# One fused two-block kernel: the first stage's projections as a stream of split weight units, x loaded first, norm sums gathered on VectorE, the memory chain placed inside the projections

## The chip, the cores and the metric

The kernel runs on one core of one Trainium2 chip. The metric is device time in microseconds (us) of one execution. The kernel works on five engines that run side by side and meet at semaphores: TensorE (PE; its weight loads are listed as PEld), VectorE (DVE), ScalarE (ACT), GpSimd (POOL) and SyncE (SP, which here only issues DMAs).

## The reference

Two transformer-like blocks follow one another on x (512 tokens x 1024). The change touches only the part of the first block ahead of its experts:

```python
mem_n = rms_norm(mem, mem_norm_w)                 # mem: 256 x 1024
h = rms_norm(x, ln1_w)
proj = h @ w_in                                   # 1024 x 2560: xr, xg, q, k, v (512 columns each)
y_rnn = recurrent_group(xr, xg, ...)              # conv of width 4, two gates, a linear recurrence, gelu gate
y_att = chunk_band_attention(q, k, v, rel_bias)   # 8 heads of 64
mixed = concat([rms_norm(y_rnn, gn_rnn_w), rms_norm(y_att, gn_att_w)])
x = x + mixed @ w_out
h = rms_norm(x, ln2_w)
# cross-attention to mem_n, 4 heads of 256: q = h @ wq, k = mem_n @ wk, v = mem_n @ wv, then @ wo
x = x + memory_cross_attention(h, mem_n, wq, wk, wv, wo)
h = rms_norm(x, ln3_w)
x = x + hierarchical_moe(h, ...)                  # 32 experts, top 2 of a group; then a final norm
# then two layers of the second block: projections, four mixers, w_out, and a feed-forward part
```

## The kernel before, in words

Activations lie transposed: features on the 128 partitions, the 512 tokens along the free dimension, so a vector of 1024 features is 8 chunks of 128x512. All weights come from DRAM in fp32.

The kernel has three stages. The first is everything up to the router, the second the experts (a loop over blocks of 128 slots), the third the two layers of the second block. The experts and the layers already multiply in split form: each fp32 weight tile and each activation is written as a high part (a copy in the fp32r type) and a low part (the difference), and three fp32r matmuls (high x high, high x low, low x high) stand for one fp32 matmul. In the layers a *unit* is 8 chunks x 256 columns of a weight (1 MB). `unit_high` (ACT, line 1201) and `unit_low` (DVE, line 1193) split it into one of two buffers `split_weights0/1` (`WHL`). `unit_high(g)` waits for the DMA of unit g and for PE to be done with unit g-2; PE waits for `weights_low` (`wl_done`) of unit g. The DMA of unit g is issued on SP once unit g-2 is split.

The first stage does none of that. It uses plain fp32 matmuls straight from the ring of three 2 MB buffers (`ring`, `first_uses`): `project` (line 1910) makes four output tiles of 128x512 from one 512-column weight block, `tokens` (line 1922) makes token-major tiles. PE's order is: stats of mem and of x, K and V of the memory (2+2 blocks), the five blocks of `w_in`, with the two gate matmuls of the recurrence (line 1945) behind each tile of the third, attention in 16 pairs (`pe_pairs`), the stats of the two group norms, `w_out`, stats, `xq`, cross-attention (`pe_attention`), `xo`, stats, router. Each stat (`pe_stats`, line 1674) multiplies all 4 or 8 squared chunks by a matrix of ones. ACT takes the results out of the banks (line 2080), squares chunks, and makes 1/root (`act_rstd`: Ln at line 2056, Exp at 2057, each with a table load). DVE does the norms (`dve_norm`, 1977), the conv, the recurrence, the softmax work and the residual adds (1983).

SP issues konst, cols, mem, two weight blocks, then x, then the other blocks, each when its ring buffer is free. POOL prepares the relative bias (through DRAM, into `AUX`) and later writes 16.8 MB of zeros to `expert_rows` (line 362), once 28 tiles are done.

Each engine works its list in order: an instruction that waits holds up all that is behind it on that engine.

Of the kernel before, what the change touches and what calls it, by code (L numbers as in the profile page):

```python
# [17 lines left out]
ALU = mybir.AluOpType  # L18
# [62 lines left out]
NORMS = [("mem", DC), ("ln1", DC), ("gn_rnn", HC), ("gn_att", HC), ("ln2", DC), ("ln3", DC), ("final", DC)]  # L81
# [28 lines left out]
def build(nc, A, out):  # L110
    with ExitStack() as ctx:
# [12 lines left out]
        with ExitStack() as places:  # L124
# [8 lines left out]
            QP = place("split_products_low", [P, 16, T])  # L133
        ring = [sb(f"ring{i}", [P, 8, 512]) for i in range(RING)]
# [31 lines left out]
        MT = S[:, 16:20, :].rearrange("p a (b m) -> p (a b) m", m=MEM)  # L166
# [3 lines left out]
        s_x = sem("x_landed")  # L170
# [4 lines left out]
        w_landed = [sem(f"weights_landed{i}") for i in range(RING)]  # L175
        act_own, dve_own, pool_own = sem("act_steps"), sem("dve_steps"), sem("pool_steps")
        sq_done, stat_done, rstd_done, h_done = sem("squares"), sem("stat"), sem("rstd_done"), sem("h_chunks")
        tile_done, tile_free = sem("tile_done"), sem("tile_free")
        xc_done, gate_done, gate_free = sem("conv_done"), sem("gates_done"), sem("gates_free")
# [5 lines left out]
        chunks_before = {}  # L185
        n = 0
        for i, (name, c) in enumerate(NORMS):
            chunks_before[name] = (i, n, c)
            n += c


        def wblock(w, j):
            return w[j]


        first_uses = [(wblock(A["xk_w"], j), tile_done, 4 * j + 4) for j in range(2)]
        first_uses += [(wblock(A["xv_w"], j), tile_done, 8 + 2 * j + 2) for j in range(2)]
        first_uses += [(wblock(A["w_in"], j), tile_done, 12 + 4 * j + 4) for j in range(5)]
        first_uses += [(wblock(A["w_out"], j), res_done, 4 * j + 4) for j in range(2)]
        first_uses += [(wblock(A["xq_w"], j), tile_done, 32 + 4 * j + 4) for j in range(2)]  # L200
        first_uses += [(wblock(A["xo_w"], j), res_done, 8 + 4 * j + 4) for j in range(2)]
        assert len(first_uses) % RING == 0
# [14 lines left out]
        for j in range(HEADS // 2):  # L217
            for t in range(TT):
# [4 lines left out]
                    bias=[AUX[:, h, T - keys:T] for h, r, tt in halves(j, t)],  # L223
# [88 lines left out]
        def wait_counted(eng, sem_, value):  # L312

            eng.wait_ge(sem_, value)
            eng.sem_inc(counted_waits, 1)

        def moe_sync(sp):
            sp.wait_ge(*first_uses[-3][1:])
            sp.wait_ge(*first_uses[-2][1:])
            sp.wait_ge(*first_uses[-1][1:])  # L320
            sp.wait_ge(slots_done, 1)
# [1935 lines left out]
```

## Time and profile before

| | us |
|---|---|
| three runs | 2636.82 median (2635.71 to 2639.95) |
| the profiled execution, whole | 2646.86 |
| its span, first to last instruction | 2645.2 |
| start to first projection matmul | 43.82 |
| last V tile done, attention begins | 243.15 |
| attention's last output copied | 313.27 |
| `w_out` done | 385.72 |
| first matmul of `xq` | 397.20 |
| `xq` done | 454.10 |
| `xo` starts | 489.82 |
| `xo` done | 545.06 |
| router starts | 561.17 |

PE is busy 88% of the span, DVE 57%, ACT 41%. The times in the lower rows are places in the chain of work that ended last, in us from the span's start. Behind the router the change only merges semaphores.

### The profile page before, as it was taken

The numbers are of one execution on the slowest core, as the hardware profiler recorded it, in microseconds if no ns is written. First come the engines' busy times: TensorE is split into PE (matmuls) and PEld (weight loads), VectorE is DVE, ScalarE is ACT, GpSimd is POOL, SyncE is SP. The second block draws the span as 40 slices with busy tenths as digits, with TensorE's granted clock in tenths as the row PEclk, the third lists the DMA queues.
The fourth block names the chain that finished last, engine by engine and source line by source line (L and its number), as shares of the span: only waits on it lengthen the run. The fifth ranks groups of instructions, "written<-read, shape, count | busy, mean of one in ns | idle before, by whom it ended". The sixth has DMA issues, their size and how long they took to land.

```text
span 2645.2 us, 26498 instructions
## 1 busy us (share of the span) xinstructions
PE 2322.3 (88%) x9824; PEld 1692.4 (64%) x9824; DVE 1507.1 (57%) x1851; ACT 1096.5 (41%) x1335; POOL 196.4 (7%) x158
## 2 busy tenths in 40 slices
PE   5998799964888888888569788999998979899997
PEld 4444444643777777776437466888877647688885
DVE  1104511233788788877556767646556785764565
ACT  2123511213666666666344564222224563422223
POOL 1000000001000000000100100211110010120110
PEclk8998799976999999999879899999999999999998
DMA  6317010006999999999612101322322101222221
GB/s 260 122 69 278 40 64 32 1 32 214 334 362 360 359 354 359 363 357 355 262 34 86 42 1 64 106 101 84 108 96 82 62 33 42 79 102 98 88 103 48
DMA packets 50454, 399.15 MB, mean 151 GB/s; under 512 B 6560, under 2 KB 7768, under 8 KB 24896
## 3 DMA queue, kind: packets, MB, share of 16 engines
q1 hardware_dynamic: 32992, 336.12, 35.3%
q0 software_dynamic: 12192, 42.97, 4.2%
q10 hardware_dynamic: 5184, 18.88, 1.7%
q8 instruction: 59, 0.97, 0.1%
q14 instruction: 27, 0.22, 0.0%
HBM read 360.15 MB, written 40.41 MB: 151 GB/s over the span
## 4 chain that ended last, share of the span: by engine, by line
PE 68%; DVE 12%; ACT 10%; issue 6%; DMA 3%; ACTq 1%; POOL 0%; SPq 0%; DVEq 0%; POOLq 0%
PE bank L987 36%; PE bank L1910 11%; PE bank L436 8%; DVE split_products L576 3%; ACT split_products L666 2%; ACT split_x_high L666 2%; PE bank L1922 2%; PE bank L1674 2%; DVE split_x_low L576 2%; PE bank L426 1%; PE bank L1704 1%; ACT S L1768 1%; PE bank L1689 1%; PE bank L1718 1%; DMA X<-in_xT 1%
## 5 line engine op out<-in xcount | busy, mean ns | idle before, releaser
L987 PE MATMUL bank<-split_x_high,split_weights 128*128 128x512 f32 x2144 | 672.9, 394 | 36.3 <-DVE split_x_low L1207 14.7
L987 PEld LDWEIGHTS bank<-split_x_high,split_weights 128*128 128x128 f32 x2144 | 408.0, 190 | 128.2 <-issue 42.7
L1201 ACT ACTIVATE split_weights<-ring 128x2048 fp32r<-128x2048 f32 (+1 forms) x92 | 170.9, 1859 | 523.2 <-PE bank L987 522.0
L987 PE MATMUL bank<-split_products,split_weights 128*128 128x512 f32 x1200 | 334.6, 395 | 4.5 <-DVE split_products L1393 4.5
L987 PE MATMUL bank<-split_x_low,split_weights 128*128 128x512 f32 x800 | 312.6, 391 | 0.0
L1910 PE MATMUL bank<-H,ring 128*128 128x512 f32 x640 | 278.1, 595 | 4.8 <-DVE H L1977 3.6
L987 PEld LDWEIGHTS bank<-split_products,split_weights 128*128 128x128 f32 x1200 | 229.3, 191 | 54.1 <-DVE split_products L1393 6.0
L1193 DVE TENSOR_TENSOR split_weights<-ring,split_weights 128x2048 fp32r<-128x2048 f32 (+1 forms) x92 | 207.9, 2260 | 94.6 <-ACT split_weights L1201 94.6
L436 PE MATMUL bank<-split_products,split_products_low 128*128 128x512 f32 x768 | 195.8, 405 | 70.2 <-DVE split_products L576 70.2
L1910 PEld LDWEIGHTS bank<-H,ring 128*128 128x128 f32 x640 | 121.9, 191 | 159.6 <-issue 155.1
L436 PEld LDWEIGHTS bank<-split_products,split_products_low 128*128 128x128 f32 x768 | 146.4, 194 | 113.6 <-DVE split_products L576 82.8
L576 DVE TENSOR_TENSOR split_products<-ring,split_products 128x2048 fp32r<-128x2048 f32 x64 | 146.7, 2292 | 109.2 <-ACT split_products L666 109.2
L436 PE MATMUL bank<-split_x_high,split_products_low 128*128 128x512 f32 x768 | 193.5, 402 | 7.0 <-DVE split_x_high L576 4.9
L436 PE MATMUL bank<-split_x_low,split_products_low 128*128 128x512 f32 x768 | 190.6, 398 | 8.5 <-DVE split_x_low L576 8.5
L666 ACT ACTIVATE split_products<-ring 128x2048 fp32r<-128x2048 f32 x64 | 122.8, 1918 | 122.0 <-DVE QKVG L588 69.4
L987 PEld LDWEIGHTS bank<-split_x_low,split_weights 128*128 128x128 f32 x800 | 151.1, 189 | 31.3
L576 DVE TENSOR_TENSOR split_x_high<-ring,split_x_high 128x2048 fp32r<-128x2048 f32 x64 | 146.5, 2289 | 40.9 <-ACT split_x_high L666 40.9
L436 PEld LDWEIGHTS bank<-split_x_high,split_products_low 128*128 128x128 f32 x768 | 145.4, 193 | 37.5 <-issue 7.6
L436 PEld LDWEIGHTS bank<-split_x_low,split_products_low 128*128 128x128 f32 x768 | 144.2, 191 | 37.6 <-DVE split_x_low L576 8.7
L965 POOL TENSOR_TENSOR QKVG<-QKVG 128x512 f32<-128x512 f32 x44 | 97.8, 2223 | 810.5 <-DVE QKVG L1407 723.9
L576 DVE TENSOR_TENSOR split_x_low<-ring,split_x_low 128x2048 fp32r<-128x2048 f32 x64 | 146.2, 2285 | 5.3 <-ACT split_x_low L666 5.3
L666 ACT ACTIVATE split_x_high<-ring 128x2048 fp32r<-128x2048 f32 x64 | 122.0, 1906 | 30.4 <-DMA ring<-in_expert_gate_w 19.8
(360 smaller groups left out, 2687.4 us busy)
## 6 DMA issues: line engine op xcount, KB each, us to landing
ring<-in_expert_gate_w SPq DMA_DIRECT2D x32, 2048.0 KB, 10.9
ring<-in_expert_up_w SPq DMA_DIRECT2D x32, 2048.0 KB, 8.8
ring<-in_expert_down_w SPq DMA_DIRECT2D x32, 2048.0 KB, 10.6
ring<-in_ffn_w_up SPq DMA_DIRECT2D x44, 1024.0 KB, 4.9
expert_rows<-nothing POOLq DMA_DIRECT2D x4, 4096.0 KB, 35.7
expert_rows<-QKVG ACTq DMA_DIRECT2D x32, 512.0 KB, 10.1
ring<-in_w_in SPq DMA_DIRECT2D x16, 1024.0 KB, 4.9
ring<-in_ffn_w_down SPq DMA_DIRECT2D x16, 1024.0 KB, 4.8
```

Of the source, the lines that this page charges most:

```text
L426: mm = pe.transpose(bank[4 + j][:, c * P:(c + 1) * P], XB[:, (4 * j + c) * P:(4 * j + c + 1) * P], ident)
L436: mm = pe.matmul(acc[j][:, :], xs[i][:, (u % 2) * n_k + k, :], w[:, n_j * k + j, :], start=(u % 2 == 0 and k == 0 and q == 0), stop=(u % 2 ...
L576: dve.tensor_tensor(e_low(u), e_raw(u), as_f32(e_high(u)), ALU.subtract).then_inc(ew_low, 1)
L666: act.activation(e_high(u), e_raw(u), ACT.Copy).then_inc(ew_high, 1)
L965: st.tell(pool.tensor_tensor(QKVG[:, 14 + i, :], QKVG[:, b, :], QKVG[:, 4 + b, :], ALU.mult), f_act)
L987: mm = pe.matmul(acc[:, :], w[:, u, k, m], x, start=first and q == 0, stop=last and q == 2)
L1193: st.tell(dve.tensor_tensor(w[:, 1, 0:ks, 0:nc_], raw_half(g)[:, :, 0:nc_], as_f32(w[:, 0, 0:ks, 0:nc_]), ALU.subtract), wl_done)
L1201: st.tell(act.activation(WHL[g % 2][:, 0, 0:ks, 0:nc_], raw_half(g)[:, :, 0:nc_], ACT.Copy), wh_done)
L1674: mm = pe.matmul(acc[:, 0:n], ones, src(c), start=(c == 0), stop=(c == chunks - 1))
L1689: pe.matmul(bank[2 * (p % 2) + i][:, 0:x["keys"]], q, k, start=True, stop=True).then_inc(s["scored"], 1)
L1910: mm = pe.matmul(b[:, 0:n], w[:, k, m * P:(m + 1) * P], src(k), start=(k == 0), stop=(k == DC - 1))
L1922: mm = pe.matmul(b[:, :], src(k)[:, t * P:(t + 1) * P], w[:, k, :], start=(k == 0), stop=(k == DC - 1))
```

## The change

All 30 MB of first-stage weights become 30 units of 256 columns (`A_UNITS`: `w_in` 10, `xk` 4, `xv` 4, `w_out` 4, `xq` 4, `xo` 4), at the head of the list of units that the layers already have. PE multiplies in three fp32r matmuls where it had one fp32 matmul. `split_unit` makes two tiles of 128x512 per unit (128x256 for the memory's K); `token_unit` makes token-major tiles, whose moving side is now the 256 columns of the unit instead of 512.

The activations are split as well: ACT copies each normed chunk (`high`), DVE subtracts (`normed_split`). x is loaded first, in four pieces; mem is loaded behind the first two units. The squares are summed on DVE (into `LN1[0]` or `SUM`), so that the matmul with ones runs over 1 to 3 chunks, not 4 or 8. K and V of the memory move behind all of `w_in`; the norm of mem, the lambda terms and `unit_high`/`unit_low` are spread over ACT's and DVE's lists. The norm of the recurrence's output is done ahead of attention. With `together=True` a unit's two tiles advance chunk by chunk as chunks are ready. Work inside attention (`inside`) takes the splitting of the recurrence's output and the square sums of the attention's. The bias goes to `H` instead of `AUX`, later (after 24 tiles); the copy of the bias in DRAM waits for 4 tiles. Semaphores of the stages are merged.

```diff
+A_UNITS = (("w_in", 10), ("xk_w", 4), ("xv_w", 4), ("w_out", 4), ("xq_w", 4), ("xo_w", 4))
@@ SP
+            for i in range(4):
+                sp.dma_start(X[:, 2 * i:2 * i + 2, :].rearrange("p a t -> p (a t)"), A["xT"][:, 2 * T * i:2 * T * (i + 1)]).then_inc(s_x[i], 16)
             sp.dma_start(konst[:, :], A["konst"]).then_inc(s_const, 16)
             sp.dma_start(cols[:, :], A["cols"]).then_inc(s_const, 16)
...
+            for g in range(UA):
+                if g >= 2:
+                    sp.wait_ge(wl_done, g - 1)
+                sp.dma_start(raw_half(g).rearrange("p k n -> p (k n)"), unit_source(g)).then_inc(half_landed[g % 2], 16)
+                if g == 1:
+                    sp.dma_start(MT.rearrange("p k m -> p (k m)"), A["memT"]).then_inc(s_mem, 16)
@@ POOL
+            pool.wait_ge(tile_done, A_XK)
+            pool.dma_start(BIAS, bass.AP(ext_copies.tensor, ...
@@ PE
+            def split_unit(g, n0, done, free, count, n=T, before=None, order=tuple(range(DC)), together=False):
+                pe.wait_ge(wl_done, g + 1)
+                w = WHL[g % 2]
...
+                def product(i, k):
+                    for q, (u, x) in enumerate(((0, hi(k)), (0, lo(k)), (1, hi(k)))):
+                        mm = pe.matmul(accs[i][:, 0:n], w[:, u, k, i * P:(i + 1) * P], x, start=(k == order[0] and q == 0), stop=(k == order[-1] and q == 2))
+                    return mm
...
+            def token_unit(g, n0, tt, hi, lo):
...
+                            mm = pe.matmul(bank[(n0 + t) % 4][:, 0:256], x[:, tok], w[:, u, k, :], start=(k == 0 and q == 0), stop=(k == DC - 1 and q == 2))
...
+            rms("ln1", ((a_add, 5, LN1[0]), (a_sq, 7, LN1[6]), (a_sq, 8, LN1[7])))
...
+            split_unit(0, **tiles(0), count=xin, before=lambda k: pe.wait_ge(a_lo, k + 1), together=True)
+            split_unit(1, **tiles(2), count=xin)
+            pe.wait_ge(side_dve, 1)
+            pe.matmul(bank[4][:, 0:MEM], ones, MSUM, start=True, stop=True).then_inc(mem_stat, 1)
+            split_unit(2, **tiles(4), count=xin)
...
+            for g in range(4, 8):
+                split_unit(g, **tiles(2 * g), count=xin)
+            token_unit(8, A_V, TT, *xin)
+            token_unit(9, A_V + TT, TT, *xin)
...
+            for u in range(4):
+                split_unit(10 + u, **tiles(A_XK + 2 * u), count=mem_in, n=MEM)
+            rms("gn_rnn", ((a_add, 8, SUM),))
+            for u in range(4):
+                token_unit(14 + u, A_XV + 2 * u, 2, *mem_in)
+            pe.wait_ge(tile_free, A_XQ)
             pe_pairs(pe, att_cfg[0], 0)
...
+            rms("gn_att", ((a_add, 10, SUM), (a_sq, 16, square[1])))
+            split_unit(18, **res(0), count=mixed, before=lambda k: pe.wait_ge(a_lo, DC + k + 1), together=True)
@@ PE, values of cross-attention
-                        pe.wait_ge(s["att_out"], outs + need)
+                    if x["t"] == 0 and u:
+                        pe.wait_ge(cross_low, outs_before(cfg, u))
@@ DVE
+            unit_low(dve, st, 2)
+            conv(0)
+            conv(1)
+            dve.wait_ge(side_act, 1)
+            st.tell(dve.tensor_reduce(MSUM, MSQ.rearrange("p k m -> p m k"), AX.X, ALU.add), side_dve)
...
+            unit_low(dve, st, 12)
+            unit_low(dve, st, 13)
+            dve.wait_ge(a_rstd, 2)
+            for c in range(HC):
+                st.tell(dve.scalar_tensor_tensor(G[:, c, :], G[:, c, :], col("gn_rnn", c), rstd[:, :], ALU.mult, ALU.mult), a_hn)
+            for g in range(14, 20):
+                unit_low(dve, st, g)
@@ ACT
+            unit_high(act, st, 10)
+            for t in range(TT):
+                evac(V[:, t, 0:256], half)
+            unit_high(act, st, 11)
+            for t in range(TT):
+                evac(V[:, t, 256:512], half)
...
+            for u in range(4):
+                unit_high(act, st, 12 + u)
+                for c in range(2 * u, 2 * u + 2):
+                    evac(KM[:, c, :], half)
+            root(1, HC)
+            for u in range(4):
+                unit_high(act, st, 16 + u)
+                for t in range(2):
+                    evac(VM[:, t, u * 256:(u + 1) * 256], half)
```

The order of instructions, at the places that matter. First the head of PE's list. Before: stats of mem (`S` times the ones in `konst`), stats of x, then the memory's K from `ring`.

```order
L1674 MATMUL bank<-S,konst 128x256 [waits squares,const_landed]
L1674 MATMUL bank<-S,konst 128x256 [waits squares] x7
L1674 MATMUL bank<-H,konst 128x512 [waits squares,rstd_done]
L1674 MATMUL bank<-H,konst 128x512 [waits squares] x7
L1910 MATMUL bank<-S,ring 128x256 [waits h_chunks,weights_landed0]
```

And after: the stats of x in three matmuls, then unit 0 chunk by chunk (six matmuls each).

```order
L1910 MATMUL bank<-S,konst 128x512 [waits x_squares_added,const_landed]
L1910 MATMUL bank<-S,konst 128x512 [waits x_squares] x2
L1876 MATMUL bank<-split_x_high,split_weights 128x512 [waits x_normed_low,weights_low]
L1876 MATMUL bank<-split_x_low,split_weights 128x512
L1876 MATMUL bank<-split_x_high,split_weights 128x512 x2
```

The stats and projections of the memory have left the head of the list. Second, DVE's list around the norm of the recurrence's output (`QKVG` times `rstd`), after; the rows with `split_weights` are `unit_low` of units 12, 13, then 14 to 19, and the last one is the first of attention.

```order
L2097 TENSOR_TENSOR ext<-ext,gatew 128x512 [waits x_squares_added,x_squares] x2
L1164 TENSOR_TENSOR split_weights<-ring,split_weights 128x2048 [waits weights_high] x2
L2106 SCALAR_TENSOR_TENSOR QKVG<-QKVG,cols,rstd 128x512 [waits x_rstd]
L2106 SCALAR_TENSOR_TENSOR QKVG<-QKVG,cols,rstd 128x512 x3
L1164 TENSOR_TENSOR split_weights<-ring,split_weights 128x2048 [waits weights_high] x6
L1713 TENSOR_TENSOR S<-bank,H 128x128 [waits scored,bias_ready]
```

Before, that place in DVE's list goes from the recurrence straight to attention.

```order
L2031 TENSOR_TENSOR S<-S 128x512 [waits root_done]
L2032 SCALAR_TENSOR_TENSOR S<-S 128x512 [waits dve_steps]
L2033 TENSOR_TENSOR QKVG<-QKVG,S 128x512 [waits dve_steps]
L1739 TENSOR_TENSOR S<-bank,AUX 128x128 [waits scored,bias_ready]
```

The wait for the root (`x_rstd`) and six splits now stand between. Third, ACT's list at the same place, after: `unit_high` of 14 and 15, K tiles of the memory out of the banks, the root, `unit_high` of 16.

```order
L1172 ACTIVATE split_weights<-ring 128x2048 [waits tile_done,half_slot_landed0]
L2189 ACTIVATE MKV<-bank 128x256 [waits tile_done] x2
L1172 ACTIVATE split_weights<-ring 128x2048 [waits tile_done,half_slot_landed1]
L2189 ACTIVATE MKV<-bank 128x256 [waits tile_done] x2
L2174 ACT_TABLE_LOAD
L2174 ACTIVATE rstd<-bank,eps 128x512 [waits x_stat]
L2175 ACT_TABLE_LOAD
L2175 ACTIVATE rstd<-rstd 128x512 [waits act_steps]
L1172 ACTIVATE split_weights<-ring 128x2048 [waits tile_done,half_slot_landed0]
```

Before, the same root stood behind attention and the squares of `QKVG`:

```order
L1785 ACTIVATE S<-bank 128x512 [waits summed]
L2113 ACTIVATE S<-QKVG 128x512 x4
L2056 ACT_TABLE_LOAD [waits h_chunks]
L2056 ACTIVATE rstd<-bank,eps 128x512 [waits stat]
```

It has moved ahead of attention and behind `unit_high(15)`, which itself waits until PE has used unit 13.

## Rows read from the trace of the kernel before

**Rows 1.** The page: busy time, share of the span, instructions.

```profile
PE 2322.3 (88%) x9824; PEld 1692.4 (64%) x9824; DVE 1507.1 (57%) x1851; ACT 1096.5 (41%) x1335; POOL 196.4 (7%) x158
```

**Rows 2.** The chain that ended last (start us, us, what), to V's tiles.

```profile
3.20 22.76 DMA X<-in_xT
...
33.81 10.01 PE bank L1674 x16
43.82 27.63 PE bank L1910 x128
71.45 27.47 PE bank L1922 x64
98.91 61.80 PE bank L1910 x144
...
215.65 27.48 PE bank L1922 x64
```

**Rows 3.** In order of time: attention's first DVE row, its last ACT row.

```profile
246.98 0.28 DVE L1739 TENSOR_TENSOR S<-bank,AUX 128x128 f32<-128x128 f32 x1
...
312.77 0.60 ACT L1785 ACTIVATE S<-bank 128x512 f32<-128x512 f32 x1 [2.10 <-PE bank L1704]
```

**Rows 4.** The chain: `w_out`, the ln2 norm's root, `xq`.

```profile
333.92 51.78 PE bank L1910 x120
...
393.64 0.69 ACT rstd L2056
394.34 1.28 ACT L2057
395.64 0.64 ACT rstd L2057
...
397.20 56.88 PE bank L1910 x128
```

**Rows 5.** The chain: cross-attention, a head's change and its end, then `xo`.

```profile
466.39 0.98 ACT H L1877 x2
...
467.51 1.13 PE bank L1822 x8
...
486.86 1.80 PE bank L1822 x16
488.68 1.09 ACT H L1877 x2
489.82 55.22 PE bank L1910 x128
```

**Rows 6.** ACT in order of time, in a layer's FFN: two unit_high.

```profile
2307.07 1.92 ACT L1201 ACTIVATE split_weights<-ring 128x2048 fp32r<-128x2048 f32 x1 [7.89 <-PE bank L987]
...
2317.95 1.92 ACT L1201 ACTIVATE split_weights<-ring 128x2048 fp32r<-128x2048 f32 x1 [4.55 <-PE bank L987]
```

**Rows 7.** Groups by line: busy, mean ns, idle ahead and its cause.

```profile
L987 PE MATMUL bank<-split_x_high,split_weights 128*128 128x512 f32 x2144 | 672.9, 394 | 36.3 <-DVE split_x_low L1207 14.7
L1201 ACT ACTIVATE split_weights<-ring 128x2048 fp32r<-128x2048 f32 (+1 forms) x92 | 170.9, 1859 | 523.2 <-PE bank L987 522.0
L1193 DVE TENSOR_TENSOR split_weights<-ring,split_weights 128x2048 fp32r<-128x2048 f32 (+1 forms) x92 | 207.9, 2260 | 94.6 <-ACT split_weights L1201 94.6
```

**Rows 8.** Durations: DVE's conv and norm in time; ACT's 256-column bank copies.

```profile
113.90 2.32 DVE L2019 SCALAR_TENSOR_TENSOR S<-S,cols 128x511 f32<-128x511 f32 x3
...
323.13 2.74 DVE L1977 SCALAR_TENSOR_TENSOR H<-QKVG,cols,rstd 128x512 f32<-128x512 f32 x4 [16.63 <-ACT rstd L2057]
...
L2080 ACT ACTIVATE MKV<-bank 128x256 f32<-128x256 f32 x8 | 3.1, 382 | 20.5 <-PE bank L1910 20.5
```

**Rows 9.** DMA issues: count, KB each, median us to landing.

```profile
ring<-in_w_in SPq DMA_DIRECT2D x16, 1024.0 KB, 4.9
expert_rows<-nothing POOLq DMA_DIRECT2D x4, 4096.0 KB, 35.7
ring<-in_xq_w SPq DMA_DIRECT2D x1, 2048.0 KB, 13.3
```

More of the change, by code:

```diff
@@ new lines, in _, with normed_split, low @@
+            for m in range(1, 6):
+                dve.wait_ge(a_sq, m + 1)
+                st.tell(dve.tensor_tensor(LN1[0], LN1[0], LN1[m], ALU.add), a_add)
+                st.wait()
+            unit_low(dve, st, 0)
+            unit_low(dve, st, 1)
+            def normed_split(stat, before, chunks, src, w, dst, lo, order=None):
+                def low(c):
+                    dve.wait_ge(a_hi, before + c + 1)
+                    d, high = lo(c)
+                    st.tell(dve.tensor_tensor(d, dst(c), high, ALU.subtract), a_lo)
+                dve.wait_ge(a_rstd, stat + 1)
+                for c in range(chunks):
+                    st.tell(dve.scalar_tensor_tensor(dst(c), src(c), w(c), rstd[:, :], ALU.mult, ALU.mult), a_hn)
+                    if c:
+                        low(c - 1)
+                low(chunks - 1)
@@ L2093, in _ @@
-            for c in range(HC):
-                evac(Q[:, c, :], full, scale=HD ** -0.5)
+            act.wait_ge(s_mem, 16)
+            st.tell(act.activation(MSQ, MT, ACT.Square), side_act)
+            unit_high(act, st, 3)
+            for c in range(2, 4):
+                evac(XR[:, c, :], full)
+            act.wait_ge(s_const, 32)
+            lam = cols[:, C1["lam"]:C1["lam"] + HC]
+            sm = lambda i: small[:, 4 * i:4 * i + 4]
+            st.do(act.activation(sm(0), lam, ACT.Abs)); st.wait()
@@ new lines, in _ @@
+            unit_high(act, st, 8)
+            for c in range(HC):
+                act.wait_ge(y_rnn, c + 1)
+                st.tell(act.activation(RG[:, c, :], RG[:, c, :], ACT.Sqrt, bias=eps[:, 2:3]), nh_done)
+            for c in range(2):
+                evac(K[:, c, :], full)
+            unit_high(act, st, 9)
+            for c in range(2, 4):
+                evac(K[:, c, :], full)
+            unit_high(act, st, 10)
+            for t in range(TT):
+                evac(V[:, t, 0:256], half)
@@ new lines, in _ @@
+            for m in range(DC):
+                if m % 2 == 0 and m:
+                    unit_high(act, st, 19 + m // 2)
+                squares(0, 2 * DC, m)
+            root(3, DC)
+            for c in range(DC):
+                high(2 * DC + c + 1, XH[:, c, :], HN[:, c, :])
+                if c == 1:
+                    unit_high(act, st, 23)
+            for u in range(4):
+                unit_high(act, st, 24 + u)
+                for c in range(2 * u, 2 * u + 2):
+                    evac(QX[:, c, :], full)
@@ L2133, in _ @@
+            act_attention(act, st, att_cfg[1])
+            for m in range(DC):
+                if m % 2 == 0 and 0 < m < 6:
+                    unit_high(act, st, 27 + m // 2)
+                squares(8, 3 * DC, m)
+            root(4, DC)
             moe_scalar(act, st)
```

585 lines of the change are left out of this document (316 added, 269 removed).

## The prediction

> **What bounds the kernel now.** I read the chain that ended last first, because the change touches one stretch only: up to the router, 561 of 2645 us. The reader should see there that PE is the chain through all projections: 43.82 to 243.13 without a hole of note [rows 2], then again 333.92 to 385.70, 397.20 to 454.08 and 489.82 to 545.04 [rows 4, 5]. Between them the chain runs through waits: x's DMA and the norms at the start [rows 2], attention from 246.98 to 313.4 [rows 3], the root of a norm [rows 4], cross-attention. PE's 88% over the whole span [rows 1] says nothing on this; in this stretch DVE and ACT are nearly idle beside PE, and that is what the change spends.
>
> **A price for the new matmul.** A layer's unit is 48 split matmuls of 512 columns, and unit_high follows unit_high by 10.88 us [rows 6]: 0.2267 us each, 0.680 for the three that replace one. The fp32 matmul is two records, 27.47/64 = 0.429 each, 0.858 together [rows 2]. So the split form takes 79% of the time, and a unit of 512-column tiles takes 10.9 us.
>
> For 256 columns the trace of before has no split matmul. A record of fp32 takes 27.63/128 = 0.216 for 2 x 256 columns and 1.80/16 = 0.1125 (with two small gaps of others in it) for 2 x 128 [rows 2, 5], each with one weight load; so columns cost 0.417 ns each, and a 128-column load hides under 0.11 us. The split stream of 512 columns pays 0.2267 - 0.2133 = 0.013 over its columns. I take 0.107 + 0.013 = 0.12 us. The bounds are 0.109 (the nearest row, no extra) and 0.227 (never dearer than twice the columns). There are 576 of them: V 192, memory K 192, memory V 192, so 69 us, bounds 63 and 131.
>
> The row shows weight loads that hide: a split matmul of 512 columns with its own load comes every 0.227 us, 0.013 above its columns. The Trainium skill (TensorE: Matmul & The Clock Gate, "Part 3: Packing small matmuls", "The mechanism") says that "LDWEIGHTS overlaps with in-flight MATMULs only when row_grp differs"; all of these use all rows, so load and columns would add. Its Part 2 gives a load as columns / 1.2, 107 ns for 128; by the two together a 256-column split matmul takes some 0.21 us, and the sum would be about 54 us worse (an estimate from that page). By that rule the 512-column stream would be at 0.32; the trace's 0.227 disagrees.
>
> **The sum, stretch by stretch** (each from the trace's places, negative is faster).
>
> Start. Before, x landed at 25.96, the mean squares ran 10.0 us on a slow PE, and the first projection began at 43.82 [rows 2]. Now x is 2 MB at the head of the queue. I estimate 10 us: by 25.96 the queue had brought x and about 5.5 MB more. Then unit 0 and 1 land by about 15 and 18, ACT splits them at 1.92 each [rows 6] and is free at 20. Root: table load 1.28, 0.69, 1.28, 0.64 = 3.9 [rows 4], to 24; the first normed, high and low chunk another 2. PE starts at 25: -18.8. Bounds 22 and 30. konst and cols are issued behind x now, 0.5 MB that PE's first stat waits for; it also waits for x's squares (8 of 0.5), which cover it. The bias has moved on POOL's queue behind tile 24; it has the memory's whole part, over 50 us, to land in before attention.
>
> Projections, before 43.82 to 243.13: 199.3. Now:
> - 8 units of w_in at 10.9: 87.2. V and the memory: 69.1. Gate matmuls 8 x 0.86 = 6.9, stats 1.3.
> - Unit 0 is paced by DVE (norm and low, 0.7 each, 16 of them) and by a PE that starts at its lower clock: +2.
> - Ahead of unit 2 PE waits for the memory's sum of squares on DVE, queued behind unit_low(2) and two convs: unit 0's end + 1.9 + 2.3 + 2 x 3.0 + 2.2 for the reduce of 2048 elements (priced as unit_low) is 12.4 against unit 1's 10.9 [rows 6 to 8]: +2.
> - unit_high(10) and (11) stand ahead of ACT's copies of the V tiles whose banks the next unit needs: 1.9 + 0.4 + a semaphore [rows 6, 8], twice: +5.
> - Ahead of unit 14 comes the largest new wait. unit_low(14) stands on DVE behind the recurrence's norm, that behind the root on ACT, that behind unit_high(15), and that waits for PE to finish unit 13. From there: high 1.9, two copies 0.8, root with table loads 3.9, four norms 2.74, low 2.3 = 11.6 [rows 4, 6 to 8], of which the stat matmul fills 0.9: +11, and 2 more since PE comes back at its lower clock.
> - The 16.8 MB of zeros go out after 28 tiles. 2 MB landed in 13.3 us beside them, against 1 MB in 4.9 alone [rows 9]. Units 15 to 17 are streamed at that time, one every 5.8 us: +3.
> Together 189.5: -9.8. For the other units the supply is hidden: high and low take 4.2 us of the 10.9 (5.8 in the memory's units), and the layers' 92 such splits spent 522 of 523 idle us waiting for PE, not PE for them [rows 7]. ACT's and DVE's other work per unit (conv 3 us each, recurrence 2.6 per chunk) fits into the rest by my count, nearest at unit 6 (2 us to spare).
>
> Attention. DVE began 3.8 us after V's last tile [rows 2, 3]; now it has unit_low(19) first: high 1.9, low 2.3 and a semaphore or two, 4.6. Inside, DVE gets six operations of 0.69 and ACT seven of 0.6. The chain alternates between the engines, so I count half: +4 (bounds 0 and 8.4). +4.8.
>
> Attention's end (313.3) to `w_out` done (385.7) was 72.4 [rows 3, 4]. Now: square 0.7, stat of two matmuls 2.4 (slow clock), root 2.7, norm, high and low 2.1, then four chunks at the pace of 1.36 and the last tile's 1.4 = 14.7 with the semaphores, less 1 because the recurrence's four chunks of unit 18 run meanwhile on PE; then three units, 32.7: 46.2. -26.2.
>
> ln2, 385.7 to 397.2: add 0.7, square 0.6, two matmuls 1.7, root 2.7, norm, high and low 2.1, 0.5 of semaphores = 8.3: -3.2.
>
> `xq`, 56.9 [rows 4]: DVE paces unit 22 (11.4), low(23) is queued behind it (+1), three units: 45.1. -11.8.
>
> Cross-attention, 35.7: unit_high(27) stands ahead of the last two copies (+2.5). At each of three changes of head PE now waits for two subtractions on DVE beyond the two copies (0.98 before [rows 5]), 1.4 us plus what DVE has in hand: +5. The last two no longer hold up `xo`, whose first six chunks are ready: -1.1. +6.4.
>
> `xo`, 55.2 [rows 5] to 43.6: -11.6. ln3, 16.1 with a stat of eight matmuls (7.1) that becomes two (1.7): -5.
>
> Sum: -18.8 - 9.8 + 4.8 - 26.2 - 3.2 - 11.8 + 6.4 - 11.6 - 5.0 = -75.2. Against the profiled execution's 2646.9 that is 2571.7. The median of the runs lies 10.0 lower, so I forecast 2561.6, say 2562.
>
> **The rivals.**
> - 256-column split matmuls are bound by their weight load, between 0.19 and 0.227 (then they cost as much as 512 columns): 576 times 0.07 to 0.107 is +40 to +62, 2602 to 2624. For it: no row has this shape. Against: fp32 records of 128 columns load once per 0.1125 us [rows 5]. Chance 8%.
> - The in-order lists bite more often than I counted: DVE has convs, recurrence and splits in one queue, and the units of the memory leave 1.6 us of slack each. With ten units late by 2 to 3 us: +20 to +30, 2582 to 2592. For it: only PE's side is measured in the layers. Chance 13%.
> - Slower than before: the two buffers don't run ahead, and each of the 30 units pays its high and low (4.4 us with semaphores) in full: +132, 2694. It decides from 75/30 = 2.5 us per unit. Against: in the layers ACT waits for PE, not the reverse [rows 7]; there the same scheme has the same 10.9 us. Chance 4%.
> - The gain is swallowed: the experts' start waits for a DMA that does not move (the zeros, the scatter), about 2637. The zeros are out by about 220 here, the router starts near 486. Chance 2%.
>
> **How the numbers follow.** The forecast with its own bounds (start +-4, attention and heads +-6, 256 columns -6) is 2545 to 2580 and holds 73%. The range takes in most of the second rival: 2545 to 2596. What a measurement can tell from no change is 0.2%, 5 us: faster 0.94, same 0.02, slower 0.04.
>
> **What would show it.** In the new profile: projections begin at 25; records of 128x512 split tiles come every 0.227 and those of 256 columns every 0.12; a hole of about 11 us on PE ahead of the memory's V, released by DVE's unit_low; two of 2.4 us at V's tiles; attention begins near 219; the router starts near 486. The forecast is wrong if the 256-column stream is slower, if PE waits for `split_weights` at most units, or if the start is not below 30 us.

## The result, and the profile after

| | before | after |
|---|---|---|
| median | 2638.39 (4 runs, 2635.71 to 2642.41) | 2563.68 (4 runs, 2560.93 to 2569.95) |
| ratio | | 0.9726, 95% interval 0.971 to 0.9742 |
| the profiled execution, whole | 2646.86 | 2563.6 |
| its span | 2645.2 | 2561.9 |
| router starts | 561.17 | 485.62 |

The forecast was 2562 in a range of 2545 to 2596; the time is 1.7 us above it. The profile answers [rows 1] with this row of its page:

```profile
PE 2225.4 (87%) x10406; PEld 1760.2 (69%) x10406; DVE 1614.1 (63%) x1937; ACT 1167.0 (46%) x1391; POOL 196.7 (8%) x158
```

PE lost 97 us of busy time, DVE gained 107 and ACT 70, and the share of PE fell by one point. That says as little as it did before. The span is 83.3 us shorter, the medians are 75 apart. Up to the router 75.55 us went (561.17 - 485.62). The other 7.75 lie behind it (2084.03 against 2076.28), where the change does nothing: they are most of the 10 us by which the profiled execution of before lay above its median. In the traces of the experiments below, none of which changes the work behind the router, that part takes 2072.7 to 2079.7, so a difference of a few microseconds in the whole time can come from there.

The chain that ended last answers [rows 2] (start us, us, what):

```profile
4.38 12.46 DMA ring<-in_w_in
...
25.11 12.70 PE bank L1876 x48
...
47.77 3.63 DVE S L2040
...
52.14 12.52 PE bank L1876 x48
...
82.43 43.53 PE bank L1876 x192
125.96 11.52 PE bank L1901 x96
137.57 1.91 ACT split_weights L1172
...
139.89 13.25 PE bank L1901 x96
153.22 1.91 ACT split_weights L1172
...
155.82 23.29 PE bank L1876 x192
179.20 1.91 ACT split_weights L1172
```

Before, PE was the chain from 43.82 to 243.13 without a hole. Now the first projection starts at 25.11. The chain leaves PE at 37.81, for the split of unit 2, two convs and the reduce (L2040, at 47.77), and again for `unit_high` at 137.57, 153.22 and 179.20. The pace in between: 43.53/192 = 0.2267 us for 512 columns as in the layers, 11.52/96 = 0.120 for the 256 columns of V, 23.29/192 = 0.121 for the memory's K.

Next, in order of time, the stretch ahead of attention (start us, us, engine, line, operation, [idle before and what ended it]):

```profile
179.20 1.91 ACT L1172 ACTIVATE split_weights<-ring 128x2048 fp32r<-128x2048 f32 x1 [3.30 <-PE bank L1876]
...
185.63 2.74 DVE L2106 SCALAR_TENSOR_TENSOR QKVG<-QKVG,cols,rstd 128x512 f32<-128x512 f32 x4 [13.71 <-ACT rstd L2175]
...
190.63 13.96 PE L1901 MATMUL bank<-split_weights,split_mixed 128*128 128x256 f32 x96 [10.66 <-DVE split_weights L1164]
...
201.15 1.91 ACT L1172 ACTIVATE split_weights<-ring 128x2048 fp32r<-128x2048 f32 x1 [15.55 <-DMA ring<-in_xv_w]
...
205.44 11.77 PE L1901 MATMUL bank<-split_weights,split_mixed 128*128 128x256 f32 x96 [0.85 <-DVE split_weights L1164]
...
214.66 1.92 ACT L1172 ACTIVATE split_weights<-ring 128x2048 fp32r<-128x2048 f32 x1 [6.70 <-DMA ring<-in_w_out]
...
223.91 0.28 DVE L1713 TENSOR_TENSOR S<-bank,H 128x128 f32<-128x128 f32 x1
```

PE stands 10.66 us ahead of unit 14. Behind that hole ACT waits for the raw units to land (`DMA` as the cause at 201.15 and 214.66), since they come beside the zeros. The DMA rows, for [rows 9]:

```profile
expert_rows<-nothing POOLq DMA_DIRECT2D x4, 4096.0 KB, 39.6
...
ring<-in_xv_w SPq DMA_DIRECT2D x4, 1024.0 KB, 8.5
```

The rest of the chain, for [rows 4, 5]:

```profile
290.97 1.13 PE bank L1910 x2
292.10 43.58 PE bank L1876 x192
335.70 0.70 DVE X L2130
...
343.37 46.55 PE bank L1876 x192
...
431.10 43.58 PE bank L1876 x192
...
485.62 13.86 PE bank L392 x64
```

`w_out`, `xq` and `xo` are now streams of 192 split matmuls at 0.227 us. Between 335.70 and 343.37 lies the ln2 norm, behind 474.68 ln3, both with a stat of two matmuls.

### The profile page after: what moved, and what is told of

Read it like the earlier page. It is cut to its first block, busy times and chain, and to the rows that moved or that the text cites. A ratio compares the mean times of both kernels' runs of the same rounds, so it can differ in the third digit from the quotient of the medians.

```text
span 2561.9 us, 27886 instructions
## 1 busy us (share of the span) xinstructions
PE 2225.4 (87%) x10406; PEld 1760.2 (69%) x10406; DVE 1614.1 (63%) x1937; ACT 1167.0 (46%) x1391; POOL 196.7 (8%) x158
## 4 chain that ended last, share of the span: by engine, by line
PE 65%; DVE 13%; ACT 11%; issue 6%; DMA 3%; ACTq 1%; POOL 0%; SPq 0%; DVEq 0%; POOLq 0%
PE bank L958 38%; PE bank L1876 9%; PE bank L430 8%; DVE split_products L570 3%; ACT split_products L659 2%; ACT split_x_high L659 2%; DVE split_x_low L570 2%; PE bank L420 1%; PE bank L1678 1%; PE bank L1663 1%; PE bank L1692 1%; PE bank L1901 1%; ACT S L1742 1%; DVE split_weights L1164 1%; ACT split_products_low L666 1%
## 5 line engine op out<-in xcount | busy, mean ns | idle before, releaser
L958 PE MATMUL bank<-split_x_high,split_weights 128*128 128x512 f32 x2144 | 672.9, 394 | 36.3 <-DVE split_x_low L1178 14.7
L1172 ACT ACTIVATE split_weights<-ring 128x2048 fp32r<-128x2048 f32 (+1 forms) x122 | 228.2, 1871 | 660.7 <-PE bank L958 521.4
L958 PEld LDWEIGHTS bank<-split_x_high,split_weights 128*128 128x128 f32 x2144 | 407.9, 190 | 128.4 <-issue 42.7
L1164 DVE TENSOR_TENSOR split_weights<-ring,split_weights 128x2048 fp32r<-128x2048 f32 (+1 forms) x122 | 276.5, 2268 | 223.1 <-ACT split_weights L1172 223.0
L1876 PE MATMUL bank<-split_x_high,split_weights 128*128 128x512 f32 x512 | 164.3, 401 | 12.4 <-DVE split_x_low L2013 7.4
L1876 PEld LDWEIGHTS bank<-split_x_high,split_weights 128*128 128x128 f32 x512 | 99.0, 193 | 36.2 <-issue 15.3
```

The lines of the kernel that those rows point to most:

```text
L958: mm = pe.matmul(acc[:, :], w[:, u, k, m], x, start=first and q == 0, stop=last and q == 2)
L1164: st.tell(dve.tensor_tensor(w[:, 1, 0:ks, 0:nc_], raw_half(g)[:, :, 0:nc_], as_f32(w[:, 0, 0:ks, 0:nc_]), ALU.subtract), wl_done)
L1172: st.tell(act.activation(WHL[g % 2][:, 0, 0:ks, 0:nc_], raw_half(g)[:, :, 0:nc_], ACT.Copy), wh_done)
L1876: mm = pe.matmul(accs[i][:, 0:n], w[:, u, k, i * P:(i + 1) * P], x, start=(k == order[0] and q == 0), stop=(k == order[-1] and q == 2))
```

## The experiments

All are edits of the changed kernel. "Router" is the start of the router's first matmul: 485.62 in the changed kernel. It is the sum of all that the change does, free of what differs behind it, and each router time is that of one profiled execution. How far a place can move by itself is seen where an edit touches nothing: the first projection lay between 25.11 and 26.04 in kernels whose edits come later, and attention, from its first DVE row to PE's last group in it, took 60.9 to 65.3 in seven kernels that have the same attention (64.5 in the changed kernel), at mean granted clocks of 0.81 to 0.71. So what an edit ahead of attention is worth is read from the start of attention, 223.91 in the changed kernel, to about a microsecond; behind it the router's time is good to some 4 us.

### The hole ahead of unit 14: two splits ahead of the wait

```diff
             unit_low(dve, st, 13)
+            unit_low(dve, st, 14)
+            unit_low(dve, st, 15)
             dve.wait_ge(a_rstd, 2)
...
-            for g in range(14, 20):
+            for g in range(16, 20):
```

> The splits of units 14 and 15 stand ahead of the wait for the root on DVE's list; nothing is left out. Theory (the 10.7 us hole ahead of the memory's V is the queue behind high(15), root and norm): PE starts unit 14 within 2 us of the stat at 180, the hole is gone, and the router starts earlier. But the zeros' 16.8 MB share the DMA engines from 173 on and units 16 to 19 are then wanted sooner, so most of the 10.7 us comes back as a wait for their DMA: router at 478 to 484 against 485.6. Rival (the hole is the whole loss, the DMA keeps up): router at 475, time 11 us below the change's 2563.7. Second rival: the hole stays, since raw unit 14 or 15 lands late: no change.

Median 2552.6, ratio to the kernel before 0.9669 (0.9644 to 0.9695); router 471.31. In order of time:

```profile
179.23 12.08 PE L1901 MATMUL bank<-split_weights,split_mixed 128*128 128x256 f32 x96
...
191.70 11.77 PE L1901 MATMUL bank<-split_weights,split_mixed 128*128 128x256 f32 x96 [0.38 <-DVE split_weights L1164]
...
201.84 1.91 ACT L1172 ACTIVATE split_weights<-ring 128x2048 fp32r<-128x2048 f32 x1 [6.29 <-DMA ring<-in_w_out]
```

The hole is gone: unit 14 starts 11.4 us earlier. It takes 12.08 instead of 13.96, with no such pause of PE before it (in the changed kernel the granted clock was 0.60 in the hole and on to 197, then 1.00). Attention starts at 211.30, 12.6 earlier. `w_out` follows its start by 66.6 instead of 68.2, which lies in attention's own spread, so of the router's 14.3 only 12.6 can be put down to the edit. The profiled execution was the fastest of the four; by the medians the gain is 11.1. That is the rival's figure, and the theory's price for the late transfers was too high. The raw units are late beside the zeros (6.29 at 201.84), but while they land PE has the second half of the memory's V to work on, so they take back little, and that only in the lead of attention: it begins 7.8 us behind V's last tile, where it was 6.7. The cause of the hole is shown: the root's wait in DVE's list, ahead of splits that did not need it.

### The zeros out of the way

```diff
-            pool.wait_ge(tile_done, 28)
+            pool.wait_ge(tile_done, 40)
```

> The 16.8 MB of zeros wait for 40 tiles (all of the memory's V) instead of 28; nothing is left out. Theory (the transfers of units 16 to 19 took 9 to 13 us beside the zeros instead of 4.8): unit 16 no longer waits, unit 19 is split 2 us after unit 17, DVE begins attention about 3 to 4 us earlier than 223.9, router at 482. The hole of 10.7 us ahead of unit 14 stays. Rival (the zeros then collide with the gathers of the experts or with attention): router as now or later, or the time behind the router grows.

Median 2561.74, ratio 0.9703 (0.9676 to 0.973); router 483.49, 2.1 us earlier, where the theory said 482. Attention begins at 221.43, 2.5 earlier, though unit 14 starts 0.8 later. The medians, 1.9 apart, can't tell this kernel from the changed one, and the time behind the router did not grow (2076.4 against 2076.3). The chain of this kernel at the memory's V:

```profile
191.46 25.74 PE bank L1901 x192
```

All four units in one piece: the hole ahead of unit 14 stays (this chain has the same root and norm ahead of it), the waits for transfers behind it are gone. The zeros' contention is real and worth 2 to 3 us by these places, and it costs in the units behind the hole, not in the hole.

### ACT's copies ahead of `unit_high`

```diff
-            unit_high(act, st, 10)
             for t in range(TT):
                 evac(V[:, t, 0:256], half)
-            unit_high(act, st, 11)
+            unit_high(act, st, 10)
             for t in range(TT):
                 evac(V[:, t, 256:512], half)
+            unit_high(act, st, 11)
...
             for u in range(4):
-                unit_high(act, st, 16 + u)
                 for t in range(2):
                     evac(VM[:, t, u * 256:(u + 1) * 256], half)
+                unit_high(act, st, 16 + u)
...
             for u in range(4):
-                unit_high(act, st, 24 + u)
                 for c in range(2 * u, 2 * u + 2):
                     evac(QX[:, c, :], full)
+                unit_high(act, st, 24 + u)
```

> ACT copies the tiles of V, of the memory's V and of xq out of the banks ahead of unit_high(10), (11), (16 to 19) and (24 to 27), instead of behind them; nothing is left out. Theory (each unit_high of 1.9 us in front of a copy that PE waits for is paid in full): the holes of 2.4 and 2.7 us ahead of units 9 and 10 go, cross-attention starts 1.9 us sooner after xq, attention too unless unit 19 is late by its DMA: 6 to 8 us in all, router at 478 to 480. Rival (the split behind the copy is then late instead, by the copies' 1.2 us, and the unit after waits for it): 0 to 3 us.

Median 2557.08, ratio 0.9687 (0.9652 to 0.9721); router 477.58, 8.0 earlier, the theory's number, but not by its parts. Its chain:

```profile
125.59 23.03 PE bank L1901 x192
148.63 23.31 PE bank L1876 x192
...
335.10 46.52 PE bank L1876 x192
...
423.07 43.57 PE bank L1876 x192
```

V runs without its two holes. From V's start to the memory's K it is 23.0 instead of 29.9 us: 5.1 of waits, and 1.7 because unit 9 had run slower behind the first of them (13.25, at a granted clock of 0.87, instead of 11.52). Attention starts 5.9 earlier, since the hole ahead of the memory's V and the late transfers stay. `w_out` is 8.3 earlier, but the 2.4 between the two lies in attention's spread (60.9 from its start to PE's last group, the shortest of all) and can't be put down to the edit. The third part of the edit brought nothing: from the end of `xq` to `xo` it is 423.07 - 381.62 = 41.45, against 431.10 - 389.92 = 41.18 in the changed kernel. There `unit_high` ahead of the last copies costs nothing that can be seen. So the edit is worth 5.9 by attention's start, and that the router came out as forecast is in part luck.

### x behind the first units

```diff
-            for i in range(4):
-                sp.dma_start(X[:, 2 * i:2 * i + 2, :].rearrange("p a t -> p (a t)"), A["xT"][:, 2 * T * i:2 * T * (i + 1)]).then_inc(s_x[i], 16)
             sp.dma_start(konst[:, :], A["konst"]).then_inc(s_const, 16)
...
                 if g == 1:
+                    for i in range(4):
+                        sp.dma_start(X[:, 2 * i:2 * i + 2, :].rearrange("p a t -> p (a t)"), A["xT"][:, 2 * T * i:2 * T * (i + 1)]).then_inc(s_x[i], 16)
```

> Undoes the order of the first loads: x is issued behind konst, cols and units 0 and 1, ahead of mem; nothing is left out. Theory (the early start comes mostly from the memory's stats, squares and projections being off the head of the chain, and unit 1 was the last to land): x's last piece lands at about 16 to 18 instead of 9.8, the root comes some 4 us later, the first projection at 29 against 25.1, all else shifts alike: router at 489 to 490. Rival (x first is what gives the start): 32 or later, near the 43.8 of the kernel before.

Median 2571.58, ratio 0.9738 (0.971 to 0.9766); router 493.53, 7.9 later. The head of its chain:

```profile
3.20 13.72 DMA X<-in_xT
...
20.69 5.47 PE bank L1910 x6
...
32.55 12.93 PE bank L1876 x48
```

The first projection starts 7.4 us later, more than the theory's 4. x is there at 16.9 instead of some 9.7 (its last piece is squared at 9.76 in the changed kernel). The two shifts agree by chance, since x's last piece is not what the changed kernel's stat waited for:

```profile
12.27 5.49 PE L1910 MATMUL bank<-S,konst 128*128 128x512 f32 x6 [12.27 <-DMA cols<-in_cols]
```

There the squares were done at 10.9, PE waited for the constants, issued behind x, until 12.27, and the root then waited 1.0 for `unit_high(1)` on ACT (18.79; the stat was done at 17.76). Here the constants come first, PE starts the stat at 20.69 behind the last sum of squares, and the root follows at 26.23.

So of the 18.7 us that the start gained, 7.4 are the order of the loads, and 11.3 the rest. Most of that rest is x too: even here it lands at 16.92, where it landed at 25.96 before, behind and beside 2 MB blocks of weights and mem. From x's landing to the first projection it is 15.6 us here and 17.9 before (15.4 in the changed kernel). The memory's stats off the head and a stat of three matmuls are therefore worth 2 to 2.5 us by these rows, and x's earlier landing about 16 of the 18.7. The theory had it the other way round; 32.55 is on the rival's side (32 or later).

### The splits inside attention, twice

```diff
                     dve.wait_ge(a_hi, DC + c + 1)
+                    st.do(dve.tensor_tensor(MIXL[c], G[:, c, :], as_f32(MIX[:, c, :]), ALU.subtract)); st.wait()
...
                 if 3 <= p < 7:
+                    act.wait_ge(a_hn, DC + p - 2)
+                    st.do(act.activation(MIX[:, p - 3, :], G[:, p - 3, :], ACT.Copy)); st.wait()
```

> Inside attention the eight operations that split the recurrence's output (four of 0.63 on ACT, four of 0.69 on DVE, in the second group of four pairs) are each done twice; the result is the same. In the changed kernel attention took 66.3 us (223.9 to 290.2), as before the change (66.4), though 13 operations were added where I had priced +4. Theory (they fall into gaps of both engines): +0 to +1 us again, router at 485.6 to 487. Rival (half of what is added lies on the chain, as predicted, and something else was saved): 5.3 us more work gives +2.5 to +3, router at 488 to 489.

One run, 2567.29; router 489.27, 3.65 later, of which 1.2 were there when attention began (225.09). The end of attention in its chain:

```profile
292.66 3.04 PE bank L1910 x4
295.71 43.56 PE bank L1876 x192
```

From attention's first DVE row to PE's last group of it: 290.69 - 225.09 = 65.6, against 288.44 - 223.91 = 64.5. From there on PE was at its lower clock: the last group took 1.97 (granted clock 0.50) instead of 1.14, and from its start to the end of the stat it was 5.0 instead of 3.7. That is the other 1.4 of the router's 3.65.

So 5.3 us of doubled work cost 1.1 there against this one trace. But the same attention without the doubled work took 60.9 to 65.3 in seven kernels, 63.5 in the mean; at about this kernel's granted clock (0.76) the three with 0.77 took 63.5 to 64.5. The doubled work then cost 1 to 2 us, between the theory and the rival, and one execution can't separate the two. It shows that the work is not paid in full: the rest would then be 60.3, below every one of the seven. That it falls in gaps of the alternating chain is the reading that fits, and is not shown. The windows of the changed kernel and of the kernel before show what the change itself added (window, its length; busy and count of PE, PEld, DVE, ACT, POOL; granted clock, DMA share, GB/s), first after, then before:

```profile
224.00:290.00 66.00, 45.23 (x298) 28.34 (x298) 48.94 (x134) 37.84 (x107) 0.00 (x0) 0.78 0.16 66
```

```profile
247.00:313.00 66.00, 46.12 (x296) 29.14 (x296) 45.20 (x129) 35.10 (x101) 0.00 (x0) 0.74 0.37 143
```

DVE carries 3.7 us more and ACT 2.7 more in the same 66 us, 6.4 together where the prediction's full price was 8.4.

### One product instead of three

```diff
-                    for q, (u, x) in enumerate(((0, hi(k)), (0, lo(k)), (1, hi(k)))):
+                    for q, (u, x) in enumerate(((0, hi(k)),)):
```

(in both kinds of unit of the first stage)

> Leaves out two of the three products (high x low and low x high) in all 30 first-stage units; splits and DMAs stay. A 512-column unit is then 16 x 0.227 = 3.6 us on PE, so what is seen is the supply. Theory (DMA, high and low of one unit overlap PE's and the other buffer's; one raw buffer turns over in 4.8 + 1.9 + 2.3 + 0.4 = 9.4 us per two units): 4.7 to 6 us per unit, router at 340 to 380, where ACT's and DVE's other work sits between. Rival (the slower case of the prediction: high and low are paid per unit behind PE): 3.6 + 4.4 = 8 us per unit, router above 410.

One run, 2464.52; router 386.62, 99 us earlier, between what the two sides said. With PE's work cut to a third, its own pace no longer hides the supply. In order of time, in `w_out`:

```profile
251.94 1.89 ACT L1172 ACTIVATE split_weights<-ring 128x2048 fp32r<-128x2048 f32 x1
253.87 2.29 DVE L1164 TENSOR_TENSOR split_weights<-ring,split_weights 128x2048 fp32r<-128x2048 f32 x1 [2.50 <-ACT split_weights L1172]
256.07 0.69 DVE L2137 TENSOR_TENSOR ext<-gatew 128x512 f32<-128x512 f32 x1
...
256.68 0.68 DVE L2130 TENSOR_TENSOR X<-X,bank 128x512 f32<-128x512 f32 x1
257.45 0.63 ACT L2292 ACTIVATE gatew<-X 128x512 f32<-128x512 f32 x1 [3.62 <-DVE X L2130]
258.12 0.69 DVE L2137 TENSOR_TENSOR ext<-ext,gatew 128x512 f32<-128x512 f32 x1 [0.76 <-ACT gatew L2292]
258.73 0.68 DVE L2130 TENSOR_TENSOR X<-X,bank 128x512 f32<-128x512 f32 x1
259.50 0.63 ACT L2292 ACTIVATE gatew<-X 128x512 f32<-128x512 f32 x1 [1.41 <-DVE X L2130]
260.04 1.89 ACT L1172 ACTIVATE split_weights<-ring 128x2048 fp32r<-128x2048 f32 x1
```

From one `unit_high` to the next, 8.1 us, without PE in it: high, low, the residual add, its square, the next add and square, and then the next high, each behind the other in the lists of ACT and DVE. So the margin of a 10.9 us unit is some 2.8 us (an estimate from these rows), not the 6.7 that 4.2 us of splitting alone would leave. In `w_in` of this kernel `unit_high` comes every 8.5 (54.94, 63.39, 71.87), there because ACT is full: the split, the copies and the conv's activations with a table load for each change. This is why the second rival did not come about in the changed kernel, and how near it lies.

### `xq` in whole fp32 matmuls

```diff
+            def whole_unit(g, n0, before=None):
...
+                w = raw_half(g)
...
+                    mm = pe.matmul(accs[i][:, :], w[:, k, i * P:(i + 1) * P], HN[:, k, :], start=(k == 0), stop=(k == DC - 1))
...
-            split_unit(22, **tiles(A_XQ), count=xq, before=lambda k: pe.wait_ge(a_lo, 2 * DC + k + 1), together=True)
+            whole_unit(22, A_XQ, before=lambda k: pe.wait_ge(a_lo, 2 * DC + k + 1))
             for u in range(1, 4):
-                split_unit(22 + u, **tiles(A_XQ + 2 * u), count=xq)
+                whole_unit(22 + u, A_XQ + 2 * u)
```

The raw units 22 to 25 are then reloaded only when PE has used them; the splits are still made.

> Undoes the split form for xq alone: its four units are multiplied as whole fp32 matmuls from the raw buffer and the unsplit normed x (nothing is left out; the splits of these units are still made, not used, and the next raw unit is loaded only when PE is done). Theory (the split form is worth 0.858 - 0.680 = 0.178 us for each of 64 matmuls, less what unit 22's pacing hid): xq takes 55 to 57 us instead of 46.6, router at 494 to 496. Rival (the gain of the stretch comes from elsewhere, the clock or the stats): xq within 4 us of 46.6.

One run, 2584.8; router 503.36. Its chain:

```profile
344.13 58.09 PE bank L1977 x128
402.28 4.77 DMA ring<-in_xo_w
407.07 1.91 ACT split_weights L1172
```

The same four units take 58.09 instead of 46.55: 11.5 us for the split form alone, on equal terms (chunk by chunk at the start in both, and the first 5 us at a granted clock of 0.50). That is the prediction's -11.8, measured within one kernel. `xq` itself began 0.8 later (344.13 against 343.37). The other 5.4 us of the router's 17.7 come from the raw buffer that PE now holds: `unit_high` ahead of the copies waits for a DMA that could only start when PE was done. The expectation had not counted that, so its router was too early. With two raw buffers of 1 MB the split form frees a buffer before PE uses the unit. This is no part of what the change gained: the kernel before, with three buffers of 2 MB, has no wait for a transfer between `xq` and cross-attention (its chain goes from 454.08 to 454.75).

### The version with all of it

The first three edits together, and the reduce of the memory's squares between the two convs instead of behind both:

```diff
             conv(0)
-            conv(1)
             dve.wait_ge(side_act, 1)
             st.tell(dve.tensor_reduce(MSUM, MSQ.rearrange("p k m -> p m k"), AX.X, ALU.add), side_dve)
+            conv(1)
```

> Puts together: splits of units 14 and 15 ahead of the wait for the root, zeros after 40 tiles, copies ahead of unit_high, and the memory's reduce between the two convs instead of behind them; nothing is left out. Theory (the effects add: -14.3 by router time for the first, -8.0 for the third, -2.1 for the second or more, since units 16 to 19 are wanted sooner, -2.8 for the reduce): router at 456 to 460, time about 2536 to 2540. Rival (the first three all shorten one stretch of 45 us, and the DMA or ACT becomes its bound): router at 465 or later.

Median 2540.21 of five executions (2534.71 to 2543.39); a sixth took 4093.42, with a mean granted clock of 0.754 against 0.946 to 0.950 in the five, and is left out, unexplained. Ratio to the kernel before 0.9624 (0.9609 to 0.9639): faster than both kernels. Router 459.02, as the theory said, though the parts that it added up were router times, with attention's spread in them. Its chain:

```profile
121.97 23.03 PE bank L1901 x192
145.00 23.29 PE bank L1876 x192
...
169.15 23.05 PE bank L1901 x192
...
265.20 43.58 PE bank L1876 x192
```

From V to the end of the memory's V there is no hole left but for the stat (0.86). Attention starts at 196.64, 27.3 earlier. The parts measured alone give 12.6 + 2.5 + 5.9 = 21.0. The reduce adds 4.0: unit 2 starts 2.4 earlier and takes 10.93 instead of 12.52. The second part is not surely the reduce's: in the first, third and fifth experiments the pause stays and unit 2 takes 10.91 to 10.94 all the same, but unit 0 took longer there (13.32 to 14.01 instead of 12.70). From the first projection to the end of unit 2 the seven kernels with the old order take 38.6 to 40.1, this one 35.4, so the reduce's place is worth 3.2 to 4.7. With 4.0 that is 25.0; the last 2.3 I have not taken apart.

## Why the prediction was right, step by step

| stretch | forecast | measured |
|---|---|---|
| first projection starts | 25 | 25.11 |
| projections, to V's last tile | 189.5 | 192.1 |
| attention begins | 219 | 223.91 |
| attention to its last output copied | 66.4 + 4 | 66.3 |
| to `w_out` done | 46.2 | 45.5 |
| ln2 | 8.3 | 7.7 |
| `xq` | 45.1 | 46.6 |
| cross-attention | 42.1 | 41.2 |
| `xo` | 43.6 | 43.6 |
| ln3 | 11.1 | 10.9 |
| router starts | 486 | 485.62 |

- *The rate.* 0.2267 for 512 columns came from [rows 6], and 0.12 for 256 columns was put together from [rows 2, 5]; the trace has 0.120 and 0.121. Undone for one matrix, it is worth 11.5 us where 11.8 were forecast.
- *The load-bound rival* is out: at 0.19 or more these 576 matmuls would have taken 40 us longer. Each of them has its own 128-column load and all rows in use. The rule of the Trainium skill (TensorE: Matmul & The Clock Gate, "Part 3: Packing small matmuls", "The mechanism"), that a load overlaps only when row_grp differs, disagrees with the trace here (0.120, where that rule would make some 0.21) as it did at 512 columns.
- *The start.* 25 was right. Of the 18.7 us about 16 are x's earlier landing and 2 to 2.5 the shorter way behind it, by the fourth experiment. konst and cols were not covered by x's squares, though I had taken them to be: PE waited for them until 12.27, 1.4 us behind the last square.
- *The reduce ahead of unit 2* was mis-sized: it took 3.63, not the 2.2 that I took from a split of as many elements. PE waited 2.76 instead of 2, and unit 2 ran 1.6 longer, at a granted clock of 0.86. 2.4 of this was not in the sum, but the 1.6 came and went between kernels with the same pause.
- *The two waits at V's tiles*: forecast +5 in all, measured 139.89 - 137.48 = 2.4 and 155.82 - 153.14 = 2.7. Not in the sum was that unit 9, behind the first of them, took 13.25 instead of 11.52. Taken away by the third experiment.
- *The hole ahead of unit 14*: forecast 11.6 from the end of unit 13, of which the stat fills 0.9, and 2 for the lower clock. Measured 190.63 - 179.11 = 11.5 with an idle time of 10.66, and 13.96 - 11.5 = 2.4. The chain in it was the one named: high, root, norm, low. The first experiment shows the cause.
- *The zeros* were mis-sized in place and in amount. I took +3 for units 15 to 17, from 13.3 us for 2 MB beside them against 4.9 for 1 MB alone, two sizes that don't compare (the 2 MB blocks of `w_in` took 8.2 in the kernel before). For 1 MB it is 9.2 to 12.7 against 4.8. Units 15 to 17 lost about 1 us. Late raw units also reached units 18 and 19, so that attention began 6.7 us after V's last tile, not 4.6 (unit 19's split waited for a DMA that took 9.97). The second experiment gives back 2.5 of it.
- *Inside attention*: forecast +4 (bounds 0 and 8.4), measured 0, from one trace on each side, where the same attention spreads over 4.4 us. Counting half of the added operations was the term that failed: half of the 6.4 us really added would be 3.2, and the mean of the seven kernels (63.5 to PE's last group) is about that of the one trace of before (63.75). The fifth experiment puts 5.3 us more at 1 to 2. Why so little is paid stays open; the gaps of the alternating chain are the likely place.
- *In-order lists biting more often*: the second rival did not happen, but the margin was 2.8 us in `w_out`, by the sixth experiment. `xq` at 46.6 is 1.5 over, and not by the terms of the sum: I had DVE pace unit 22 and hold up unit 23 (+1), but PE does not wait once in it. After the 5.08 us in which it stood for the norm it runs at a granted clock of 0.50 until about 349, and 43.5 us of stream become 46.6 (a row as in the fifth experiment's windows):

```profile
346.00:349.00 3.00, 3.00 (x8) 2.31 (x7) 3.00 (x6) 1.27 (x3) 0.00 (x0) 0.50 0.00 0
```

- *Cross-attention*: +2.5 for `unit_high(27)` ahead of the copies was too much. Moving it brought nothing, and the stretch came out 0.9 shorter than forecast.

So three stretches were forecast short (projections by 2.6, the lead of attention by 2.1, `xq` by 1.5) and others long (inside attention by 4.1, cross-attention by 0.9, `w_out` and the norms by 1.5), and they cancel within half a microsecond at the router. The misses are some 6 us on either side, within the forecast's own range of 2545 to 2580; that it came within 2 us is in good part luck, the more so as the same attention differs by up to 4.4 us from one kernel's trace to another's.

## What to carry to other kernels

Moving work into streams pays where the sum says so, but look at each in-order list for a wait that stands ahead of work which does not need it. Three such orders here (splits behind a norm's root, copies behind a split, a reduce behind two convs) cost about a third of what the change gained, and each was mended by moving a few lines. When a rate is forecast from matmuls of another shape, take the columns' price and the overhead apart, as two rows allow. And before trusting that a supply is hidden, count the whole loop between two supplies through all engines' lists, not the splitting alone: 8.1 us here, not 4.2.

## What the hardware showed that I had not expected

- A sum over 8 chunks read with a stride (128 x 256 results from 2048 elements each row) took 3.63 us on DVE, where a subtraction of 2048 adjacent elements takes 2.29.
- 1 MB loads took 4.8 us alone, and 9.2 to 12.7 beside the 16.8 MB of zeros, while 399 GB/s moved over 180 to 224; with the zeros later, the waits for them were gone.
- The same attention took 60.9 to 65.3 us in seven kernels, 60.9 and 63.0 at a mean granted clock of 0.81, 65.3 at 0.71.
- After a pause of PE the cost can be more than the pause: the granted clock was 0.60 from 180 to 197, and the matmuls behind the hole took 2.4 us more. Behind the 2.4 us ahead of unit 9 it was 1.7 more. At the end of attention the 16 matmuls of the last group took 1.14 or 1.15 in four kernels and 1.97 or 1.98 in five, with the same instructions.
- In the 256-column stream the weight loads were busy 22.98 of 23.00 us (169 to 192 in the last kernel), as PE was. The columns alone are worth 0.107 us of the 0.120 (an estimate from the 0.417 ns per column of the fp32 records). Whether loads or columns set the last 0.013 is open.
